# A transformer block pair on one core: the first mixer's projections in a new order

## The chip, the cores and the metric

The program runs on one core of a Trainium2 chip. The metric is the device time of one execution in microseconds; for the kernel before, the median of three runs is 1390.18 us (1381.83 to 1393.23). The engines are PE (matrix products), DVE and ACT (element-wise work), POOL, and SP, which here issues all loads. Each engine works through its own list in order and waits on semaphores where a list says so.

## The reference

512 tokens of width 1024 pass two blocks. The first block is a hybrid mixer, a cross attention to 256 memory rows and a convolutional feed-forward; the second has four small mixers and an MLP. The change lies in the hybrid mixer alone:

```python
def hybrid_mixer(x, w_in, ..., w_out):
    proj = x @ w_in
    ml_qk, ml_v, ml_o, ml_i, ml_f, sw_q, sw_k, sw_v = jnp.split(proj, IN_SPLITS, axis=-1)
    ml_qk = jax.nn.silu(causal_dwconv(ml_qk, ml_conv_w, ml_conv_b))
    ml_q, ml_k = jnp.split(ml_qk, 2, axis=-1)
    h_ml = mlstm(ml_q, ml_k, ml_v, ml_o, ml_i + ml_i_bias, ml_f + ml_f_bias, ml_norm_g)
    h_sw = sliding_window_attention(sw_q, sw_k, sw_v, swa_sinks, rel_bias)
    return jnp.concatenate([h_ml, h_sw], axis=-1) @ w_out
```

The mLSTM has 4 heads of width 128 with an input and a forget gate per head and token. The sliding window has 8 query heads of width 64 on 2 key heads; it works in 4 blocks of 128 tokens, each looking at itself and the block before, with a bias table of 128 x 8 x 256. A softmax with a sink stands in the middle.

## The kernel before

All weights come in 221 chunks of 128 x 1024 fp32 (512 KB). A chunk is loaded into one of 3 stage slots (SP), its high part is cast to fp32r (ACT, `split`, L1023), the rest is subtracted (DVE, `split`, L1377), and a product of fp32 quality is three fp32r products: high x high, high x low, low x high. There are 6 slots for split chunks. A load of chunk i waits for the low part of chunk i-3 (its stage slot), the cast of chunk i for the product of chunk i-6. The tokens are split the same way into `xh` and `xl`, 8 pieces of 128 features (`x_in`).

A class `Plan` writes one list of steps; each engine's program walks this list and does its part of each step. The order in `Plan.mixer_one` is thus the order on every engine. `fill` takes one of 8 PSUM banks in turn and PE waits for whoever read it last; `out` gives it back; `pump` appends `split` steps for up to six chunks ahead. `feat` is one chunk with weights stationary and 512 tokens moving (24 products); `tok_small` and `tok_half` have tokens stationary. `sliding_window` and `mlstm` are generators whose pieces are laid between chunks, one at each `next(side)`.

Names in the order of the list: `in_a` (the sliding window's k, q, and as sixth chunk the 8 gate rows, padded to 128), `in_sv` (its v), `in_qk` (q and k of the mLSTM, 8 chunks), `in_v`, `in_o`, `kv_k` and `kv_v` (the memory's keys and values), `out1` (the output projection). For a window block n: `swa_scores` (PE scores; DVE adds bias and takes the maximum; ACT exponentials), `swa_norm` (DVE), `swa_turn` (PE transposes the probabilities, ACT copies), `swa_pv` (PE product with v). For a chunk of q or k: `conv_qk` (ACT copies and scales, DVE three taps) and `silu_qk`. For a head: `ml_gate` and `ml_score` (PE, then ACT and DVE), `ml_out` (PE), `ml_norm` (DVE, one step on POOL), `ml_turn` (PE). `masks` waits on DVE for the bias table. `tok_full` lays out `out1`: for each of 8 chunks the four token tiles, the last five chunks tile by tile (`tail`).

Of the kernel before, what the change touches and what calls it, by code (L numbers as in the profile page):

```python
# [18 lines left out]
CH = 1024  # L19
# [13 lines left out]
WEIGHTS = [("in_a", 6), ("in_sv", 1), ("in_qk", 8), ("in_v", 4), ("in_o", 4), ("kv_k", 8), ("kv_v", 8), ("out1", 8),  # L33
           ("xq", 8), ("xo", 8), ("up", 44), ("down", 22), ("in2_c", 4), ("in2_a", 4), ("in2_v", 2), ("in2_b", 10),
           ("out2", 8), ("m1", 32), ("m2", 32)]
CHUNKS = [(n, c) for n, k in WEIGHTS for c in range(k)]
CHUNK0 = {n: CHUNKS.index((n, 0)) for n, _ in WEIGHTS}


class Plan:  # L40
# [66 lines left out]
    def tok_full(self, name, nk, early=1):  # L107
        for b in range(8):
# [7 lines left out]
        for k in range(7):  # L116
            split_in(k)
        ahead = 7
        for k in range(nk - TAIL):
            self.need()  # L120
            self.step("full", name, k)
            self.used += 1
            self.pump()
            if k + 7 < nk:
# [46 lines left out]
    def sliding_window(self):  # L171
# [9 lines left out]
        yield  # L181
        for n in range(4):
            self.step("swa_norm", n)
            for _ in range(3):
                yield
# [12 lines left out]
            yield  # L198

    def mlstm(self):  # L200
# [9 lines left out]
        def turned(h):  # L210
            self.fill("ml_t", h)
            self.step("ml_turn", h)
            self.out(("ml_t", h), "ml_y", h + 1)
            if h == 0:
                self.step("first", "out1")

# [4 lines left out]
        for h in range(4):  # L221
            if h:
                turned(h - 1)
# [8 lines left out]
            if h < 2:  # L232
                front(h + 2)
                yield
        yield
        turned(3)

    def mixer_one(self):
        for k in range(8):
            if k in (0, 5, 7):  # L240
                self.pump(1)
# [3 lines left out]
        for j in self.feat("in_a", 6):  # L245
            self.step("in_a", j)
            self.out(("in_a", j), *(("a_out", j + 1) if j < 5 else ("g_in", 2)))
        self.tok_small("in_sv", 0)
        self.step("in_sv")
        self.out(("in_sv", 0), "sv_out", 1)  # L250
        self.pump()
        self.step("gates")
        side = self.sliding_window()
        for j in self.feat("in_qk", 8):
# [4 lines left out]
            if j == 2:  # L259
                self.fill("gate_columns")  # L260
                self.step("gate_columns")
                self.out(("gate_columns",), "gc_out", 1)
            next(side, None)
        self.step("silu_qk", 7)
        self.tok_half("in_v", 0, 4, lambda: next(side, None))
        for t in range(4):
            self.out(("in_v", 0, t), "v_out", t + 1)
        self.step("in_v")
        for k in self.feat_mid("in_o", 4, lambda: next(side, None)):
            self.step("in_o", k)  # L270
            self.out(("in_o", k), "o_t", k + 1)
            next(side, None)
        for _ in side:
            pass
        self.step("ml_setup")
        side = self.mlstm()
# [3 lines left out]
        next(side)  # L280
        for k in self.feat("kv_k", 8):
            self.step("kv_k", k)
            self.out(("kv_k", k), "kt_out", k + 1)
            next(side, None)
        for hf in range(2):
            self.tok_half("kv_v", hf, 2, lambda: next(side, None))
            for t in range(2):
                self.step("kv_v", hf, t)
                self.out(("kv_v", hf, t), "vm_out", 2 * hf + t + 1)
                next(side, None)  # L290
        for _ in side:
            pass
        self.step("x_again")
        self.step("rows", "ln1")
        self.tok_full("out1", 8)
# [260 lines left out]
class Own:  # L556
# [16 lines left out]
    ["st0", "st1", "st2"] + [f"ld_x{k}" for k in range(4)]  # L573
# [3 lines left out]
    + ["mm", "tile_done", "swa_s_full", "swa_t_full", "swa_o_full", "gc_full", "ml_m_full", "ml_s_full", "ml_h_full",  # L577
# [3 lines left out]
    + ["w_hi", "x_hi", "f_hi", "a_own", "a_out", "sv_out", "gate_e", "gate_x", "swa_e", "swa_pt", "swa_y", "qk_u", "qk_y",  # L581
# [5 lines left out]
    + ["w_lo", "x_lo", "f_lo", "v_own", "masks", "ones", "pad", "g_in", "gate_p", "gate_a", "gate_m", "gate_f", "gc_out",  # L587
# [8 lines left out]
def build_program(nc, d, out):  # L596
    plan = Plan()
    with ExitStack() as ctx:
# [35 lines left out]
        th = reg(22, 512)  # L634
# [10 lines left out]
        pad0 = reg(84, 520, 2064)  # L645
# [9 lines left out]
        sel = gb[:, 1, 0:512]  # L655
        gi = gb[0:4, 1, 512:1024]
        ones = gb[0:4, 2, 0:512]
        g3 = gb[0:4, 2, 512:1024]
        sw_mx, sw_nm, sw_sm, sw_es, sw_rr = (st[:, 8 * i:8 * i + 8] for i in range(5))
# [58 lines left out]

        def tile_ready(name, t):
# [11 lines left out]
        def _(e):  # L731
# [9 lines left out]
            def by_weights(b, i, cols, ks):  # L741
# [3 lines left out]
                for k in ks:  # L745
                    if i == 0:
                        q.wait_ge(S["x_lo"], plan.x_at["x", k])
# [5 lines left out]
            def feat(name, j, x, part=None):  # L753
# [4 lines left out]
                if i:  # L758
                    q.wait_ge(S["x_lo"], x)
# [11 lines left out]
            def feat_rest(name, j, x, part=None):  # L771
# [3 lines left out]
                if part != "front":  # L775
                    last.then_inc(S["mm"])

# [53 lines left out]
            def full(name, k):  # L831
                for t in range(4):
                    last = product(name, k, t)
                last.then_inc(S["mm"])
# [34 lines left out]
            def swa_scores(n):  # L869
                lo = 0 if n else 128  # L870
                q.wait_ge(S["a_out"], 5)
                for j in range(2):
                    rows = slice(64 * j, 64 * j + 64)
                    for ip in range(2):
                        b = tiles(fill("swa_score", n, 2 * j + ip)[:], 2)
                        for i in range(2):
                            last = e.matmul(b[:, i, lo:256], swq[rows, 2 * ip + i, tok(n)],
                                            swk[rows, (n - 1) * 128 + lo:(n + 1) * 128], start=True, stop=True)
                        last.then_inc(S["swa_s_full"])

            def swa_turn(n):
                q.wait_ge(S["ld_ident"], 16)
                q.wait_ge(S["swa_p"], n + 1)
                for j in range(2):
                    for kb in ([0, 1] if n else [1]):
                        b = fill("swa_turn", n, j, kb)
                        for i in range(4):
                            last = e.transpose(b[:, tok(i)], L[:, 4 * j + i, tok(kb)], ident[:])
                        last.then_inc(S["swa_t_full"])

            def swa_pv(n):
                b = fill("swa_pv", n)
                q.wait_ge(S["swa_pt"], 4 * n + 2)
                q.wait_ge(S["sv_out"], 1)
# [7 lines left out]
            def ml_gate(h):  # L902
                b = fill("ml_m", h)
                q.wait_ge(S["gate_m"], 1)
                q.wait_ge(S["ld_masks"], 80)
                e.matmul(b[:], sel[0:4, tok(h)], g3, start=True, stop=True).then_inc(S["ml_m_full"])

            def ml_score(h):
                q.wait_ge(S["qk_s"], 5 + h)
# [5 lines left out]
            def ml_out(h):  # L915
                E = Es[h % 2]
                q.wait_ge(S["v_out"], 4)
                q.wait_ge(S["ones"], 1)
# [85 lines left out]
            mine = dict(feat=feat, feat_half=feat_half, feat_rest=feat_rest, tok_small=tok_small, tok_half=tok_half,  # L1004
# [9 lines left out]
        def _(e):  # L1014
# [3 lines left out]
            def split(i):  # L1018
# [4 lines left out]
                e.copy(whi[:, i % NSPLIT, :], stage[:, s, :]).then_inc(S["w_hi"])  # L1023

            def x_in(k):
                q.wait_ge(S[f"ld_x{k // 2}"], 32)
# [7 lines left out]
            def x_from(name, k):  # L1034
                q.wait_ge(S["mm"], CHUNK0[name] + max(0, k - 7))
                if name == "out1":
                    q.wait_ge(S["ml_y" if k < 4 else "swa_y"], k + 1 if k < 4 else 4)
# [7 lines left out]
                e.copy(xh[:, k % 8, :], source[name][:, k, :]).then_inc(S["x_hi"])  # L1045

            def first_in(name):
# [3 lines left out]
                if name == "out1":  # L1051
                    q.wait_ge(S["ml_y"], 1)
# [6 lines left out]
                e.copy(first[:, 0, :], source[name][:, 0, :]).then_inc(S["f_hi"])  # L1059
# [8 lines left out]

            def in_a(j):
                if j < 5:  # L1070
                    q.wait_ge(S["mm"], CHUNK0["in_a"] + j + 1)
# [961 lines left out]
```

## Time and profile before

| what | us |
|---|---|
| median of 3 runs | 1390.18 |
| profiled execution | 1390.49 |
| its span in the trace | 1388.7 |
| PE busy | 1335.8 |
| DVE busy | 737.9 |
| ACT busy | 548.0 |
| out1 begins (PE) | 251.13 |

The span is what the engines' records cover; what lies around it is 1.8 us. A busy share of 96% on PE says that nearly all time is a list of products, but the records of pipelined products overlap, so their cost is read from one start to the next and not from their length. The granted clock of PE is 1.00 (2.4 GHz) or 0.50 (1.2 GHz) in a stretch.

### The profile page before, as it was taken

Reading aid. Unit: us, or ns where it says so; the run is one execution under the profiler, and the core shown is the slowest. Engines: PE = TensorE matmul, PEld = TensorE weight load, DVE = VectorE, ACT = ScalarE, POOL = GpSimd, SP = SyncE. Lnnn points to the kernel's source line nnn. Section 1 sums busy time; section 2 is a strip of 40 time slices with the busy share of each in tenths; the row PEclk is TensorE's granted clock in tenths of the full one; section 3 lists DMA queues with packets and bytes.
Section 4 is the critical chain, followed back from the end, with each engine's and each line's share of the span. In section 5 each row is a group of like instructions: output and inputs, shape, how many; then the busy total and the mean of one; then the engine's idle time right before and its main releaser. Section 6 shows DMA issues by size and latency. Waiting matters only on the chain.

```text
span 1388.7 us, 15947 instructions
## 1 busy us (share of the span) xinstructions
PE 1335.8 (96%) x6476; PEld 1100.2 (79%) x6476; DVE 737.9 (53%) x1049; ACT 548.0 (39%) x908; POOL 7.8 (1%) x8
## 2 busy tenths in 40 slices
PE   6999998999999999999999989998989999999997
PEld 5877786888688888888888788765778888888886
DVE  4486577482537655555533679765373333433323
ACT  3455642323413544444422242476343322323221
POOL 0000001000000000000000000000000000000000
PEclk9999999999999999999999989999999999999999
DMA  7322223623112432323432132111223323333211
GB/s 258 118 77 76 83 70 99 219 77 107 46 46 76 122 91 91 104 94 105 139 105 92 31 124 92 52 55 62 90 76 105 93 93 105 107 105 93 92 60 61
DMA packets 37096, 131.55 MB, mean 95 GB/s; under 512 B 4252, under 2 KB 4892, under 8 KB 36768
## 3 DMA queue, kind: packets, MB, share of 16 engines
q1 hardware_dynamic: 37024, 130.55, 29.2%
q8 instruction: 51, 0.84, 0.2%
q14 instruction: 21, 0.17, 0.1%
HBM read 128.43 MB, written 2.10 MB: 94 GB/s over the span
## 4 chain that ended last, share of the span: by engine, by line
PE 81%; DVE 9%; ACT 5%; issue 2%; DMA 1%; POOL 0%; SPq 0%; DVEq 0%; ACTq 0%; POOLq 0%
PE bank L748 14%; PE bank L749 14%; PE bank L750 14%; PE bank L824 5%; PE bank L825 5%; PE bank L826 5%; PE bank L829 5%; PE bank L827 5%; PE bank L828 5%; DVE wlo L1377 1%; ACT whi L1023 1%; PE bank L958 1%; DVE R L1485 1%; DVE xl L1407 1%; PE bank L788 1%
## 5 line engine op out<-in xcount | busy, mean ns | idle before, releaser
L1377 DVE TENSOR_TENSOR wlo<-stage,whi 128x1024 fp32r<-128x1024 f32 x221 | 269.4, 1224 | 338.6 <-ACT whi L1023 338.6
L748 PE MATMUL bank<-xh,whi 128*128 128x512 f32 (+1 forms) x1152 | 424.3, 368 | 23.4 <-DVE xl L1407 12.0
L749 PE MATMUL bank<-xl,whi 128*128 128x512 f32 (+1 forms) x1152 | 418.1, 363 | 0.0
L750 PE MATMUL bank<-xh,wlo 128*128 128x512 f32 (+1 forms) x1152 | 417.9, 363 | 0.0
L1023 ACT CAST whi<-stage 128x1024 fp32r<-128x1024 f32 x221 | 229.7, 1045 | 242.3 <-PE bank L829 195.7
L748 PEld LDWEIGHTS bank<-xh,whi 128*128 128x128 f32 x1152 | 221.1, 192 | 66.0 <-DVE xl L1407 13.4
L750 PEld LDWEIGHTS bank<-xh,wlo 128*128 128x128 f32 x1152 | 221.0, 192 | 33.2
L749 PEld LDWEIGHTS bank<-xl,whi 128*128 128x128 f32 x1152 | 221.2, 192 | 32.4 <-issue 1.2
L824 PE MATMUL bank<-whi,xh 128*128 128x512 f32 x296 | 116.2, 392 | 0.1
L826 PE MATMUL bank<-wlo,xh 128*128 128x512 f32 x296 | 115.2, 389 | 0.0
L825 PE MATMUL bank<-whi,xh 128*128 128x512 f32 x296 | 115.2, 389 | 0.0
L829 PE MATMUL bank<-whi,xl 128*128 128x512 f32 x296 | 115.2, 389 | 0.0
L827 PE MATMUL bank<-wlo,xh 128*128 128x512 f32 x296 | 115.2, 389 | 0.0
L828 PE MATMUL bank<-whi,xl 128*128 128x512 f32 x296 | 115.2, 389 | 0.0
L1814 DVE TENSOR_TENSOR R<-bank,R 128x512 f32<-128x512 f32 x32 | 22.1, 692 | 96.5 <-ACT R L1350 96.5
L1350 ACT ACTIVATE R<-bank 128x512 f32<-128x512 f32 x32 | 19.1, 598 | 118.6 <-PE bank L750 118.6
L1658 DVE SCALAR_TENSOR_TENSOR R<-R,par 128x512 f32<-128x512 f32 x44 | 33.1, 751 | 60.7 <-ACT R L1206 60.4
L824 PEld LDWEIGHTS bank<-whi,xh 128*128 128x128 f32 x296 | 55.6, 188 | 12.0 <-issue 0.8
L828 PEld LDWEIGHTS bank<-whi,xl 128*128 128x128 f32 x296 | 55.6, 188 | 11.6
L827 PEld LDWEIGHTS bank<-wlo,xh 128*128 128x128 f32 x296 | 55.6, 188 | 11.6
L825 PEld LDWEIGHTS bank<-whi,xh 128*128 128x128 f32 x296 | 55.6, 188 | 11.5 <-issue 0.2
L829 PEld LDWEIGHTS bank<-whi,xl 128*128 128x128 f32 x296 | 55.6, 188 | 11.5
(247 smaller groups left out, 1389.5 us busy)
## 6 DMA issues: line engine op xcount, KB each, us to landing
stage<-in_W_m SPq DMA_DIRECT2D x64, 512.0 KB, 3.5
stage<-in_W_up SPq DMA_DIRECT2D x44, 512.0 KB, 3.5
stage<-in_W_down SPq DMA_DIRECT2D x22, 512.0 KB, 3.5
stage<-in_W_out SPq DMA_DIRECT2D x16, 512.0 KB, 3.6
stage<-in_W_in_a SPq DMA_DIRECT2D x10, 512.0 KB, 3.7
stage<-in_W_in_b SPq DMA_DIRECT2D x10, 512.0 KB, 3.4
stage<-in_W_in_qk SPq DMA_DIRECT2D x8, 512.0 KB, 4.3
stage<-in_W_kv_k SPq DMA_DIRECT2D x8, 512.0 KB, 3.5
```

Of the source, the lines that this page charges most:

```text
L748: e.matmul(b[:, cols], hi[:, k, :], xh[:, k, cols], start=(k == 0), stop=False)
L749: e.matmul(b[:, cols], hi[:, k, :], xl[:, k, cols], start=False, stop=False)
L750: last = e.matmul(b[:, cols], lo[:, k, :], xh[:, k, cols], start=False, stop=(k == 7))
L824: e.matmul(b[0][:], a_hi, hi[:, 0:512], start=(k == 0), stop=False)
L825: e.matmul(b[1][:], a_hi, hi[:, 512:1024], start=(k == 0), stop=False)
L826: e.matmul(b[0][:], a_hi, lo[:, 0:512], start=False, stop=False)
L827: e.matmul(b[1][:], a_hi, lo[:, 512:1024], start=False, stop=False)
L828: e.matmul(b[0][:], a_lo, hi[:, 0:512], start=False, stop=end)
L829: return e.matmul(b[1][:], a_lo, hi[:, 512:1024], start=False, stop=end)
L1023: e.copy(whi[:, i % NSPLIT, :], stage[:, s, :]).then_inc(S["w_hi"])
L1377: e.tensor_tensor(wlo[:, i % NSPLIT, :], stage[:, i % NSTAGE, :], whi[:, i % NSPLIT, :].bitcast(F32), ALU.subtract).then_inc(S["w_lo"])
L1658: e.scalar_tensor_tensor(out=y, in0=u[:, 0:512], scalar=P("fcw", w), in1=y, op0=ALU.mult, op1=ALU.add).then_inc(own.inc())
```

## The change

1. v of the mLSTM, the 8 gate columns and the sliding window's v become one product `tokv` at the very start: 8 chunks of 648 columns (324 KB), tokens stationary, two groups of 264 and 384 columns for each of 4 token tiles, all 8 banks. PE does the high parts first and waits for the low parts later. Of chunks 0 to 2 the loads go between the first token pieces.
2. The gates come out with tokens on partitions; four transposes (`gate_turn`) turn them. The gate product of each head takes an fp32r high and low part in one product of 36 rows, and no longer an fp32 product of 4 rows.
3. q and k come head by head (0, 4, 1, 5, ...), with two buffers each for conv and tanh.
4. The sliding window is taken apart in halves of four heads (`swa_norm n j`, `swa_turn n j`), the scores alternate between the two row halves, and its pieces are laid twice in each `in_qk` chunk. The mLSTM's pieces begin within `in_o`.
5. The memory is loaded after the last silu. `out1` takes the window's rows first; the fourth token tile of its first three chunks comes after the other three tiles, with the last head's transposes between.

The names in the listings: `tokv_out` evicts the first product (ACT v of heads 0, 1 and gates; DVE the rest); `w_lo`, `w_hi` count split chunks, `st0` to `st2` landings, `swa_e` exponentials, `swa_p` normalised halves.

ACT at the end of the first product, in the change. L1112 is the cast of a chunk, L1162 and L1164 the two copies of `tokv_out`, L1169 the copy of `in_a 0`:

```order
L1112 CAST whi<-stage 128x1024 [waits mm,st0]
L1112 CAST whi<-stage 128x1024 [waits mm,st1]
L1162 COPY R<-bank 128x2x128 [waits vt_full]
L1164 COPY R<-bank 128x2x4 [waits gate_z]
L1162 COPY R<-bank 128x2x128 [waits vt_full]
L1164 COPY R<-bank 128x2x4
L1162 COPY R<-bank 128x2x128 [waits vt_full]
L1164 COPY R<-bank 128x2x4
L1162 COPY R<-bank 128x2x128
L1164 COPY R<-bank 128x2x4
L1169 COPY R<-bank 128x512 [waits mm]
```

The casts of chunks 12 and 13 (the first two rows) stand ahead of the first copy; before, none of these copies was there, and v was copied from its banks much later.

DVE from block 1's logits to its first half of normalised probabilities, before (L1456 logits, L1377 low part of a chunk, L1485 conv, L1494 silu, L1471 to L1475 normalisation):

```order
L1456 SCALAR_TENSOR_TENSOR R<-bank,R 128x512 [waits swa_s_full] x3
L1460 TENSOR_REDUCE st<-R 128x8 [waits swa_logit]
L1462 TENSOR_TENSOR st<-st,gb 128x8 [waits v_own]
L1464 TENSOR_SCALAR st<-st 128x8 [waits v_own]
L1466 TENSOR_TENSOR st<-gb,st 128x8 [waits swa_nm]
L1377 TENSOR_TENSOR wlo<-stage,whi 128x1024 [waits w_hi,st0]
L1485 SCALAR_TENSOR_TENSOR R<-R,par 128x512 [waits qk_y,qk_u]
L1485 SCALAR_TENSOR_TENSOR R<-R,par 128x512 [waits v_own] x2
L1494 SCALAR_TENSOR_TENSOR R<-R 128x512 [waits qk_t]
L1471 TENSOR_TENSOR st<-st 128x8 [waits swa_e]
L1473 RECIPROCAL st<-st 128x8 [waits v_own]
L1475 TENSOR_TENSOR R<-R,st 128x2048 [waits v_own]
```

The same in the change (L1566 logits, L1474 low part, L1596 conv, L1606 silu, L1582 to L1586 normalisation, here from the second half's maximum):

```order
L1574 TENSOR_SCALAR st<-st 128x4 [waits v_own]
L1576 TENSOR_TENSOR st<-gb,st 128x4 [waits swa_nm]
L1474 TENSOR_TENSOR wlo<-stage,whi 128x1024 [waits w_hi,st2]
L1596 SCALAR_TENSOR_TENSOR R<-R,par 128x512 [waits qk_y,qk_u]
L1596 SCALAR_TENSOR_TENSOR R<-R,par 128x512 [waits v_own] x2
L1606 SCALAR_TENSOR_TENSOR R<-R 128x512 [waits qk_t]
L1474 TENSOR_TENSOR wlo<-stage,whi 128x1024 [waits w_hi,st0]
L1582 TENSOR_TENSOR st<-st 128x4 [waits swa_e]
L1584 RECIPROCAL st<-st 128x4 [waits v_own]
L1586 TENSOR_TENSOR R<-R,st 128x1024 [waits v_own]
L1596 SCALAR_TENSOR_TENSOR R<-R,par 128x512 [waits qk_y,qk_u]
L1596 SCALAR_TENSOR_TENSOR R<-R,par 128x512 [waits v_own] x2
```

One chunk with its conv and silu still lies between, and now a second chunk's low part too; maxima and normalisation are in halves.

PE around the first transposes of block 1, in the change (L976 transposes, L966 scores, L986 product with v):

```order
L803 MATMUL bank<-xl,whi 128x512
L804 MATMUL bank<-xh,wlo 128x512
L976 MATMUL bank<-ident,R 128x128 [waits swa_p]
L976 MATMUL bank<-ident,R 128x128 x3
L976 MATMUL bank<-ident,R 128x128 [waits swa_logit]
L976 MATMUL bank<-ident,R 128x128 x3
```

Before, the same transposes came four chunks after the scores, now two; the wait is for the first half alone now.

The diff, cut to its core:

```diff
-WEIGHTS = [("in_a", 6), ("in_sv", 1), ("in_qk", 8), ("in_v", 4), ("in_o", 4), ...
+WEIGHTS = [("tokv", 8), ("in_a", 5), ("in_qk", 8), ("in_o", 4), ...
+WIDTH = {"tokv": 648}
+VG = [slice(0, 264), slice(264, 648)]
+QK = [0, 4, 1, 5, 2, 6, 3, 7]
...
     def tok_full(self, name, nk, early=1, late=7, lag=0, between=None):
...
+            if k < lag:
+                self.need(k)
+                if k == lag - 1:
+                    between()
+                self.step("full", name, k, range(3))
+                if k < lag - 1:
+                    continue
...
+                for o in range(lag):
+                    self.step("full", name, o, range(3, 4))
+                    self.used += 1
+                    self.pump()
+                continue
...
     def sliding_window(self):
...
         scores(0)
-        yield
         for n in range(4):
-            self.step("swa_norm", n)
-            for _ in range(3):
-                yield
+            yield
+            yield
+            self.step("swa_norm", n, 0)
+            yield
+            self.step("swa_norm", n, 1)
             for j in range(2):
...
-            self.step("swa_turn", n)
-            yield
+                self.step("swa_turn", n, j)
+                if j == 0:
+                    yield
             if n < 3:
                 scores(n + 1)
+            yield
             self.fill("swa_pv", n)
...
     def mixer_one(self):
+        for t in range(4):
+            for g in range(2):
+                self.fill("tokv", t, g)
+        for k in range(NSPLIT):
+            self.pump(1)
             self.step("x_in", k)
             self.x_split("x", k)
         self.step("masks")
+        for k in range(8):
+            self.step("tokv", k)
+            self.used += 1
+            self.pump(1)
+            if k + NSPLIT < 8:
+                self.step("x_in", k + NSPLIT)
+                self.x_split("x", k + NSPLIT)
+        for t in range(4):
+            self.step("tokv_out", t)
...
+        for j in self.feat("in_a", 5):
             self.step("in_a", j)
+            if j == 0:
+                self.fill("gate_turn")
+                self.step("gate_turn")
...
+        next(side)
+        for j in self.feat_mid("in_qk", 8, lambda: next(side, None)):
             self.step("conv_qk", j)
...
+        self.step("mem_load")
+        sides = [side]
...
+        sides.append(self.mlstm())
+        for k in self.feat_mid("in_o", 4, mid):
...
-        self.tok_full("out1", 8)
+        self.tok_full("out1", 8, 1, 6, 3, lambda: self.ml_turned(3))
...
+            def tokv(k):
+
+                hi, lo = whi[:, k % NSPLIT, :], wlo[:, k % NSPLIT, :]
+                groups = [(t, g) for t in range(4) for g in range(2)]
+                q.wait_ge(S["w_hi"], k + 1)
+                q.wait_ge(S["x_hi"], plan.x_at["x", k])
+                for t, g in groups:
+                    b = fill("tokv", t, g) if k == 0 else bank_of("tokv", t, g)
+                    n = VG[g].stop - VG[g].start
+                    e.matmul(b[:, 0:n], xh[:, k, tok(t)], hi[:, VG[g]], start=(k == 0), stop=False)
+                q.wait_ge(S["w_lo"], k + 1)
...
+                q.wait_ge(S["x_lo"], plan.x_at["x", k])
...
             def swa_scores(n):
...
+                for ip in range(2):
+                    for i in range(2):
+                        for j in range(2):
+                            rows = slice(64 * j, 64 * j + 64)
+                            b = tiles(bank_of("swa_score", n, 2 * j + ip)[:], 2)
...
             def ml_gate(h):
                 b = fill("ml_m", h)
-                e.matmul(b[:], sel[0:4, tok(h)], g3, start=True, stop=True).then_inc(S["ml_m_full"])
+                e.matmul(b[:], selr[:, tok(h)], gsum, start=True, stop=True).then_inc(S["ml_m_full"])
...
+            def tokv_out(t):
+                b = bank_of("tokv", t, 0)
+                q.wait_ge(*tokv_ready(t))
+                e.copy(vaug[:, t, 0:2, 0:128], tiles(b[:, 0:256], 2))
+                q.wait_ge(S["gate_z"], 1)
+                e.copy(gt[:, t, :].rearrange("p (g c) -> p g c", g=2)[:, :, 0:4], tiles(b[:, 256:264], 2)
+                       ).then_inc(S["v_out"])
...
+            def mem_load():
+                q.wait_ge(S["qk_s"], 8)
                 e.dma_start(MT, d["memT"]).then_inc(S["ld_mem"], 16)
```

## Rows read from the trace of the kernel before

**Rows 1.** The page, busy time and share of the span by engine.

```profile
PE 1335.8 (96%) x6476; PEld 1100.2 (79%) x6476; DVE 737.9 (53%) x1049; ACT 548.0 (39%) x908; POOL 7.8 (1%) x8
```

**Rows 2.** Windows: length, busy us (instructions) by engine, PEclk, DMA share, GB/s.

```profile
0.00:10.00 10.00, 2.43 (x6) 1.98 (x7) 3.72 (x5) 4.60 (x6) 0.20 (x4) 1.00 0.83 288
0.00:57.00 57.00, 46.32 (x242) 38.81 (x243) 23.06 (x25) 20.45 (x27) 0.20 (x4) 1.00 0.64 220
57.00:171.00 114.00, 112.27 (x540) 88.00 (x538) 77.47 (x106) 63.32 (x140) 0.00 (x0) 1.00 0.24 74
171.00:251.00 80.00, 72.88 (x426) 61.19 (x425) 54.69 (x133) 31.17 (x57) 7.62 (x4) 0.96 0.31 98
225.50:232.20 6.70, 5.96 (x26) 5.88 (x27) 2.95 (x9) 0.00 (x0) 0.00 (x0) 0.50 0.44 143
```

**Rows 3.** Timeline of PE, 0 to 57: start, us, line, idle before.

```profile
7.57 0.77 PE L748 MATMUL bank<-xh,whi 128*128 128x512 f32 x1 [7.57 <-DVE xl L1383]
...
10.27 0.45 PE L748 MATMUL bank<-xh,whi 128*128 128x512 f32 x1
...
45.94 0.22 PE L788 MATMUL bank<-whi,xh 128*128 128x128 f32 x1
...
56.60 0.45 PE L748 MATMUL bank<-xh,whi 128*128 128x512 f32 x1
```

**Rows 4.** Timeline of SP (DMA issues), 15 to 36.

```profile
18.57 0.43 SPq L1853 DMA_DIRECT2D R<-in_swbias  x1
29.43 0.33 SPq L1840 DMA_DIRECT2D stage<-in_W_in_sv  x1
```

**Rows 5.** Timeline of DVE, 14 to 32.

```profile
25.94 2.29 DVE L1413 TENSOR_TENSOR R<-R,gb 128x2048 f32<-128x2048 f32 x1 [9.71 <-DMA R<-in_swbias]
```

**Rows 6.** Timeline of ACT, 33 to 37.

```profile
34.40 1.05 ACT L1023 CAST whi<-stage 128x1024 fp32r<-128x1024 f32 x1 [13.68 <-DMA stage<-in_W_in_sv]
```

**Rows 7.** Timeline of PE, products of 512 and of 256 columns.

```profile
108.34 0.39 PE L803 MATMUL bank<-whi,xh 128*128 128x512 f32 x1
...
119.00 0.39 PE L805 MATMUL bank<-whi,xl 128*128 128x512 f32 x1
...
182.05 0.28 PE L748 MATMUL bank<-xh,whi 128*128 128x256 f32 x1
...
184.45 0.28 PE L750 MATMUL bank<-xh,wlo 128*128 128x256 f32 x1
```

**Rows 8.** Timeline of PE, scores of block 1, gate product of head 0.

```profile
93.05 2.96 PE L877 MATMUL bank<-R 64*128 64x256 f32 x16
...
171.16 1.12 PE L906 MATMUL bank<-gb 4*128 4x512 f32 x2
172.21 1.13 PE L912 MATMUL bank<-R 128*128 128x512 f32 x2
```

**Rows 9.** Timeline of DVE through block 1 of the sliding window.

```profile
101.77 2.48 DVE L1456 SCALAR_TENSOR_TENSOR R<-bank,R 128x512 f32<-128x512 f32 x4
104.28 2.29 DVE L1460 TENSOR_REDUCE st<-R 128x8 f32<-128x2048 f32 x1
...
112.67 1.23 DVE L1377 TENSOR_TENSOR wlo<-stage,whi 128x1024 fp32r<-128x1024 f32 x1 [5.50 <-ACT whi L1023]
113.84 2.33 DVE L1485 SCALAR_TENSOR_TENSOR R<-R,par 128x512 f32<-128x512 f32 x3
...
117.12 2.29 DVE L1475 TENSOR_TENSOR R<-R,st 128x2048 f32<-128x2048 f32 x1
```

**Rows 10.** Timeline of ACT, exponentials of block 1 and the cast behind them.

```profile
107.01 0.51 ACT L1090 ACTIVATE R<-R,st 128x256 f32<-128x256 f32 x1 [7.86 <-DVE st L1464]
...
110.97 0.19 ACT L1093 ACTIVATE st<-st 128x8 f32<-128x8 f32 x1
...
111.53 1.04 ACT L1023 CAST whi<-stage 128x1024 fp32r<-128x1024 f32 x1
```

**Rows 11.** Timeline of PE, the wait before ml_turn of head 2.

```profile
226.24 1.08 PE L932 MATMUL bank<-ident,R 128*128 128x128 f32 x4 [3.55 <-DVE R L1563]
```

More of the change, by code:

```diff
@@ L31 @@
 NPAR = _o
-WEIGHTS = [("in_a", 6), ("in_sv", 1), ("in_qk", 8), ("in_v", 4), ("in_o", 4), ("kv_k", 8), ("kv_v", 8), ("out1", 8),
+WEIGHTS = [("tokv", 8), ("in_a", 5), ("in_qk", 8), ("in_o", 4), ("kv_k", 8), ("kv_v", 8), ("out1", 8),
            ("xq", 8), ("xo", 8), ("up", 44), ("down", 22), ("in2_c", 4), ("in2_a", 4), ("in2_v", 2), ("in2_b", 10),
@@ L105, in tok_half, with tok_full @@
             self.pump()
-    def tok_full(self, name, nk, early=1):
-        for b in range(8):
+    def tok_full(self, name, nk, early=1, late=7, lag=0, between=None):
+        for b in range(6 if lag else 8):
             self.fill(name, b)
@@ L114, in split_in @@
                 self.x_split(name, k)
-        for k in range(7):
+        for k in range(late):
             split_in(k)
-        ahead = 7
+        ahead = late
         for k in range(nk - TAIL):
+            if k < lag:
[5 more added lines that the diff above has]
+                    continue
+                while ahead < min(nk, 8):
+                    split_in(ahead)
+                    ahead += 1
+                self.fill(name, 6)
+                self.fill(name, 7)
+                for o in range(lag):
[3 more added lines that the diff above has]
+                continue
             self.need()
-            self.step("full", name, k)
+            self.step("full", name, k, range(4))
             self.used += 1
             self.pump()
-            if k + 7 < nk:
+            if ahead <= k + 7 < nk:
                 split_in(k + 7)
@@ L233, in mlstm, with ml_turned @@
                 front(h + 2)
+                if h == 1:
+                    self.step("first", "out1")
                 yield
-        yield
-        turned(3)
-    def mixer_one(self):
-        for k in range(8):
-            if k in (0, 5, 7):
-                self.pump(1)
+            elif h == 2:
+                yield
+            if h < 3:
+                self.ml_turned(h)
+    def ml_turned(self, h):
+        self.fill("ml_t", h)
+        self.step("ml_turn", h)
+        self.out(("ml_t", h), "ml_y", h + 1)
+    def mixer_one(self):
+        for t in range(4):
[3 more added lines that the diff above has]
+            self.pump(1)
             self.step("x_in", k)
@@ L258, in mixer_one, with mid @@
                 self.step("silu_qk", j - 1)
[L259 to L262, printed above, removed]
             next(side, None)
         self.step("silu_qk", 7)
[L265 to L269, printed above, removed]
+        self.step("ml_setup")
+        self.step("mem_load")
+        sides = [side]
+        def mid():
+            for s in sides:
+                if next(s, "end") != "end":
+                    return
+        sides.append(self.mlstm())
+        for k in self.feat_mid("in_o", 4, mid):
             self.step("in_o", k)
             self.out(("in_o", k), "o_t", k + 1)
[L272 to L276, printed above, removed]
+            mid()
         for k in range(2):
@@ L283, in mixer_one @@
             self.out(("kv_k", k), "kt_out", k + 1)
-            next(side, None)
+            mid()
         for hf in range(2):
-            self.tok_half("kv_v", hf, 2, lambda: next(side, None))
+            self.tok_half("kv_v", hf, 2, mid)
             for t in range(2):
@@ L289, in mixer_one @@
                 self.out(("kv_v", hf, t), "vm_out", 2 * hf + t + 1)
-                next(side, None)
-        for _ in side:
-            pass
+        for s in sides:
+            for _ in s:
+                pass
         self.step("x_again")
         self.step("rows", "ln1")
-        self.tok_full("out1", 8)
+        self.tok_full("out1", 8, 1, 6, 3, lambda: self.ml_turned(3))
         self.step("warm", 0)
@@ L829, in product, with full @@
                 return e.matmul(b[1][:], a_lo, hi[:, 512:1024], start=False, stop=end)
-            def full(name, k):
-                for t in range(4):
+            def full(name, k, some):
+                for t in some:
                     last = product(name, k, t)
-                last.then_inc(S["mm"])
+                if 3 in some:
+                    last.then_inc(S["mm"])
             def tail(name, nk, t):
@@ L1058, in first_in @@
                     q.wait_ge(S["cf_y"], 1)
[L1059 removed]
+                e.copy(first[:, 0, :], source_of(name, 0)).then_inc(S["f_hi"])
             def turn(name, t):
```

314 lines of the change are left out of this document (171 added, 143 removed).

## The prediction

> **What bounds the kernel now.** I read the page first, for the busy shares: PE is busy in 1335.8 of 1388.7 us, DVE in 737.9, ACT in 548.0 [rows 1]. Then the windows by stage, to see where PE is not busy [rows 2]: 10.7 us of the first 57, 1.7 of the next 114 (to the end of the sliding window), 7.1 of the 80 with the mLSTM, and there it also ran 6.7 us at a granted clock of 0.50 (1.2 of 2.4 GHz). So the first mixer, to 251 us, is PE work of about 224 us plus waits; behind it nothing moves. The change is worth what PE work it removes, and which waits go and come. For those I read the timelines of PE at the start [rows 3], of SP, DVE and ACT where the bias table lands [rows 4 to 6], and of DVE and ACT through one block of the sliding window [rows 9, 10].
>
> **PE work.** A 512-column product takes 0.227 us from start to start (47 steps in 10.66), a 256-column one 0.120 (20 steps in 2.40) [rows 7], a 128-column one 0.111 (96 from 45.94 to 56.60) [rows 3]. Removed: the gates' chunk and v, 24 + 96 products of 512 columns, 27.2 us, and sv, 10.7. Added: 96 of 264 and 96 of 384 columns; on the line between 0.120 and 0.227 these are 0.123 and 0.173, together 28.5 (ends: all at 0.120, 23.0; all at 0.227, 43.6; the widths lie nearer the lower end). Four small transposes add 0.45. Sum **-9.0**.
> The Trainium skill, "TensorE: Matmul & The Clock Gate", section "Back-to-back issue gap", gives N/2.4 + 2.5 ns from start to start; by it the removed work is 31.3 us, the added 26.4, and this term -4.9 in place of -9.0. The rows for 128 and 512 columns are dearer than it, and I go by the rows.
> The gate product of each mLSTM head was two fp32 records, 1.05 us (171.16 to 172.21) [rows 8]; as one fp32r pass of 512 columns it is 0.23: four times 0.82, **-3.3**. The scores' products now alternate between the two halves of the rows; 16 records took 2.96 us [rows 8]. At best that halves, at worst nothing; I take the half for the three full blocks, since the two halves of the rows share nothing but the queue (each product of a pair writes its own bank): **-4.5**, end 0.
>
> **Start.** PE waited until 7.57 for a 512 KB chunk and two token pieces, then 3.1 us more in three waits for data or low parts [rows 2]. Now the first product needs 324 KB and 256 KB and only the high parts; the data lands at about 4.2, the casts (0.7 + 0.6) end at 5.1. Each piece of the sum over k then has 3.6 us of PE work against 580 KB, some 2 us of transfer at the 288 GB/s of the first 10 us [rows 2], so PE stays fed through k = 7. Gain 2.5 + 3.1. The half clock at the start (products 0.43 apart until 10.27, 1.2 us lost) begins earlier and lasts, I take, 1 us more: **-4.6**. The token product then ends at 5.1 + 28.5 + 2 = about 35.5.
>
> **A new wait behind it.** All eight banks are taken, so in_a 0 needs the ACT copy of the first bank, and in ACT's order this stands behind the cast of chunk 13. That chunk's load waits for the low part of chunk 10, chunk 10's load for the low part of chunk 7, and that stands on DVE behind the bias add, which waits for its 1 MB. It was issued at 18.57 and the add began at 25.94, with the 1 MB of memory ahead of it [rows 4, 5]. Now it is issued about 19.4 with that gone: 24.2. Add 2.3 and memsets: 26.9; low parts of chunk 6 and 7 with their tokens: 29.4; chunk 10 lands 33.3, its low part is done at 35.6; chunk 13 lands 39.3, cast 40.4, copies 41.0. PE waits 5.7 us (ends: 3, if the bias lands at 22; 8, if each landing takes the 5.0 from 29.43 to 34.40 [rows 4, 6]). After the wait of 3.55 at 226.24, PE had a half clock and lost half of 5.96 busy us [rows 2, 11]; here I take 2.5. **+8.2**.
>
> **The sliding window, packed into in_qk.** Before, a block spread over about five steps of one chunk each; now over 2.5 chunks. From the end of scores 1 to the moment PE wants its probabilities lie 4 half chunks and one product with v: 10.9 + 1.0 = 11.9 us. The chain on DVE and ACT: 2.0 of conv and silu still queued; logits 2.48; two half reductions with three small steps each, 3.3; the last four exponentials, 2.1 (eight took 3.96, 107.01 to 110.97); the cast 1.04 behind them [rows 9, 10]; DVE had nothing to do meanwhile, 5.5 us in the row of 112.67 and about 3.4 now. Then low part 1.2, ACT's evictions for conv 0.6, conv 2.3, silu 0.6, another low part 1.15, half a normalisation 1.6. Sum 18.6: PE waits **6.7**. The old rows check the method: 101.77 to 119.41 is 17.6 with the same pieces. For blocks 2 and 3 the PE leg is 12.8 and the chain 18.1 and 18.4: 5.3 and 5.6. For block 0 (128 columns) 8.2 against 11.7: 3.5. That is 21.1; after the three longer waits the half clock costs 6 more, less than three times 3.0 since it covers part of a later wait. **+27**, ends 0 (DVE never late) and +36. The 1.7 us idle of 57 to 171 go: **-1.5**.
>
> **mLSTM.** Its steps now begin in in_o. From ml_out to ml_turn lie 11 to 12 us of PE for heads 0 and 1, 8.9 for head 2, and all of kv_v and three chunks of out1 for head 3; the chain of ml_norm was about 9 (217 to 226.24). So 7.1 idle and 3.0 of half clock go: **-10.1**. Small waits for the in_a copy and the later memory load: +0.9. out1 has the same products in another order; its chunks 6 and 7 are cast after tile 3's first products, 1.4 us apart, with 4 us of other chunks before they are needed: 0. The gates' chain on ACT (about 12 us) lies beside in_a 1 and 2, whose low parts exist: 0.
>
> **Sum.** -9.0 - 3.3 - 4.5 - 4.6 + 8.2 + 27 - 1.5 - 10.1 + 0.9 = +3.1 on the profiled execution's 1390.5, so 1393.6; that execution is 0.3 over the median of 1390.18, so I say **1393**. What the change gains in work and at the mLSTM it gives back in the sliding window.
>
> **Rivals.** (A) PE never waits in the sliding window: the halves of scores and normalisation shorten the chain, and DVE has work of about 19 us a block against 18.9 of PE. For it: equal work; against it: order, since DVE stands still behind the casts on ACT whatever its load. 1393 - 27 = 1366; with half the waits 1379. (B) The other side, slower: the half clock. It decides if 0.50 stays granted for the whole leg from a block's first transposes to the next scores, 6.2 us of PE, and not for a part: three legs at 6.2 more in place of 2 each, +12.6, 1406. For it: the waits come every 25 us and open with small work; against it: after 226.24 the clock was back within 6.7 us. (C) The added products cost 0.227 whatever their width: +15, 1408; the 256-column row speaks against it. (D) The start's wait does not come, the bias being early: 1385.
>
> **Numbers.** Forecast with D 0.59, A and its half 0.26, B 0.12, C 0.03. Runs shown lie within 0.8%, so 1% (14 us) is about the least that counts as a change: below 1376 faster, above 1404 slower. Faster 0.26, same 0.60, slower 0.14. The range takes in most of A's half and B: 1368 to 1406; the forecast's own is 1383 to 1401.
>
> **What would show it.** First matmul near 5.1; a PE wait before in_a 0 near 35 to 41, released by ACT; four waits of 3 to 7 us at the first transposes of a block, released by the probabilities on DVE; DVE idle 3 to 4 us behind the cast of a chunk; out1's first product at 251 + 3 = 254. The forecast is wrong if these four waits are under 2 us each (A), or if PE's clock is at 0.50 for more than 25 us before 254 (B).

## The result, and the profile after

The changed kernel took **1406.9 us** (median; runs 1403.33, 1405.70, 1408.17) against 1390.9 for the kernel before on the same chip (1381.83 to 1393.23): ratio **1.0119, 95% interval 1.0078 to 1.0161**, 16 us slower. One more run of the changed kernel, of 2432 us, was disturbed and is in no ratio. The forecast was 1393 (1368 to 1406), "within 1%" at 0.60. It was wrong: the time lies 0.9 us outside the range, on the slow side, and the first mixer lost 18.4 us where 3 were forecast.

The profiled execution took 1408.17 us, 17.7 more than the profiled one before. Where the difference lies is one row: the first product of `out1`, at 251.13 before, forecast at 254.

```profile
PE 1331.3 (95%) x6452; PEld 1101.4 (78%) x6452; DVE 745.5 (53%) x1091; ACT 549.2 (39%) x919; POOL 7.8 (1%) x8
...
269.53 0.39 PE L910 MATMUL bank<-whi,first 128*128 128x512 f32 x1
```

It is 18.4 us later, so all of the loss is ahead of it in the first mixer; counted from there, the last product comes 0.8 us earlier than before. PE's busy time alone [rows 1] would say the opposite: it fell by 4.5 us. The windows show where PE stood (columns as in [rows 2]; the last one is a stretch of half clock that begins in the last long wait and outlasts it):

```profile
0.00:38.00 38.00, 31.81 (x192) 31.26 (x192) 16.19 (x23) 13.39 (x19) 0.20 (x4) 1.00 0.66 219
...
75.00:190.00 115.00, 96.36 (x437) 71.91 (x436) 73.16 (x129) 56.23 (x141) 0.00 (x0) 0.90 0.20 66
190.00:270.00 80.00, 71.49 (x436) 63.43 (x435) 52.77 (x126) 29.66 (x49) 7.62 (x4) 0.94 0.34 106
205.40:215.60 10.20, 4.95 (x23) 4.97 (x24) 4.49 (x6) 3.44 (x6) 0.00 (x0) 0.50 0.17 53
```

Before, 57 to 171 had 1.7 us of idle PE; now 75 to 190 has 18.6. The waits of PE up to `out1` (engine, line, what it waited for; sum, times, longest) name them:

```profile
PE bank L976 <- DVE R L1586: 18.5, 4, 6.1
PE bank L802 <- ACT R L1164: 8.4, 1, 8.4
PE bank L802 <- issue: 7.7, 1, 7.7
PE bank L840 <- ACT xh L1116: 5.1, 1, 5.1
PE bank L845 <- DVE wlo L1474: 1.0, 1, 1.0
PE bank L1021 <- DVE R L1675: 0.8, 1, 0.8
```

The first row is the four waits in the sliding window, the second the wait before `in_a 0`: both were forecast. The third, **7.7 us before `kv_k 0`**, was not. The fourth is the start (forecast 5.1), the fifth a gap inside the first product, the last the one wait left at `ml_turn`.

### The wait that was not forecast

PE at `kv_k 0`. L1000 is the scores of head 2, L802 the first product with the memory:

```profile
200.11 0.50 PE L994 MATMUL bank<-first 36*128 36x512 f32 x1
200.54 2.42 PE L1000 MATMUL bank<-R 128*128 128x512 f32 x8
210.66 0.55 PE L802 MATMUL bank<-xh,whi 128*128 128x256 f32 x1 [7.69 <-issue]
211.01 0.41 PE L803 MATMUL bank<-xl,whi 128*128 128x256 f32 x1
```

The releaser reads "issue", so the row names nobody; one has to look for who wrote `xh` and `xl` last. ACT in the same stretch (L1239 and L1241 are head 2's exponentials, L1121 the memory's two casts into `xh`):

```profile
203.66 0.40 ACT L1239 ACTIVATE R<-R,st 128x128 f32<-128x128 f32 x1 [2.85 <-DVE R L1622]
203.97 0.56 ACT L1241 ACTIVATE R<-bank,st 128x384 f32<-128x384 f32 x1
...
205.92 1.04 ACT L1112 CAST whi<-stage 128x1024 fp32r<-128x1024 f32 x1
206.85 2.00 ACT L1121 CAST xh<-R 128x1024 fp32r<-128x1024 f32 x2
```

And DVE (L1675 the last part of head 0's `ml_norm`, L1622 the first of head 2's weights, L1487 the memory's low parts):

```profile
201.58 1.11 DVE L1675 TENSOR_SCALAR R<-R,st 128x128 f32<-128x128 f32 x4 [0.91 <-POOL st L2027]
202.61 0.42 DVE L1611 TENSOR_SCALAR R<-R 128x512 f32<-128x512 f32 x1
202.94 0.68 DVE L1622 TENSOR_TENSOR R<-bank,gb 128x512 f32<-128x512 f32 x1
204.56 1.82 DVE L1632 SCALAR_TENSOR_TENSOR R<-bank,R 128x512 f32<-128x512 f32 x4 [0.94 <-ACT R L1241]
207.06 1.23 DVE L1474 TENSOR_TENSOR wlo<-stage,whi 128x1024 fp32r<-128x1024 f32 x1 [0.67 <-ACT whi L1112]
208.20 2.35 DVE L1487 TENSOR_TENSOR xl<-R,xh 128x1024 fp32r<-128x1024 f32 x2
```

The last product that reads the tokens in `xh` starts at 199.79. The casts of the memory into it could follow at once; they start 7 us later, because the plan puts head 2's gate and scores ahead of `mem_in`. ACT stands 2.85 us for a DVE instruction behind a normalisation and POOL's step, then runs the exponentials and a weight cast. The load had nothing to do with it: issued at 168.07, it took 5.6 us. `kv_k 0` then ran at 0.213 per 256-column product where the kernel before has 0.120 [rows 7], 2.3 us more.

### The two forecast places

ACT behind the first product and DVE at the bias add (answers to [rows 5, 6]):

```profile
44.83 1.04 ACT L1112 CAST whi<-stage 128x1024 fp32r<-128x1024 f32 x1 [1.91 <-DMA stage<-in_W_in_qk]
45.78 0.37 ACT L1162 COPY R<-bank 128x256 f32<-128x256 f32 x1
46.04 0.17 ACT L1164 COPY R<-bank 128x8 f32<-128x8 f32 x1
```
```profile
28.24 2.29 DVE L1510 TENSOR_TENSOR R<-R,gb 128x2048 f32<-128x2048 f32 x1 [9.95 <-DMA R<-in_swbias]
```
```profile
37.50 0.34 PE L851 MATMUL bank<-whi,xl 128*128 128x384 f32 x1
46.26 0.79 PE L802 MATMUL bank<-xh,whi 128*128 128x512 f32 x1 [8.43 <-ACT R L1164]
```

The banks are full and done at 37.8, but the two copies that free the first stand behind the cast of chunk 13, whose load hangs, by the stage slots, on a low part behind the bias add.

DVE through block 1 of the window (answers to [rows 9]):

```profile
98.94 1.28 DVE L1566 SCALAR_TENSOR_TENSOR R<-bank,R 128x512 f32<-128x512 f32 x2
...
104.96 0.16 DVE L1576 TENSOR_TENSOR st<-gb,st 128x4 f32<-128x4 f32 x1
108.18 1.23 DVE L1474 TENSOR_TENSOR wlo<-stage,whi 128x1024 fp32r<-128x1024 f32 x1 [3.06 <-ACT whi L1112]
109.83 2.33 DVE L1596 SCALAR_TENSOR_TENSOR R<-R,par 128x512 f32<-128x512 f32 x3 [0.42 <-ACT R L1218]
112.07 0.68 DVE L1606 SCALAR_TENSOR_TENSOR R<-R 128x512 f32<-128x512 f32 x1
112.67 1.22 DVE L1474 TENSOR_TENSOR wlo<-stage,whi 128x1024 fp32r<-128x1024 f32 x1
...
114.21 1.22 DVE L1586 TENSOR_TENSOR R<-R,st 128x1024 f32<-128x1024 f32 x1
```

The chain is the one that was added up: 3.06 us idle behind a cast that stands behind the exponentials, then two low parts, a conv and a silu ahead of the normalisation. PE's four waits show as steps from one start to the next of 3.31, 6.46, 4.57 and 5.76; less the 0.23 of the product in each step they are 3.1, 6.2, 4.3 and 5.5, in sum 19.2. (The view of the waits has 18.5, since it counts from the modelled end of the product before.)

### The profile page after: what moved, and what is told of

Read it like the earlier page. It is cut to its first block, busy times and chain, and to the rows that moved or that the text cites. A ratio compares the mean times of both kernels' runs of the same rounds, so it can differ in the third digit from the quotient of the medians.

```text
span 1406.4 us, 15979 instructions
## 1 busy us (share of the span) xinstructions
PE 1331.3 (95%) x6452; PEld 1101.4 (78%) x6452; DVE 745.5 (53%) x1091; ACT 549.2 (39%) x919; POOL 7.8 (1%) x8
## 4 chain that ended last, share of the span: by engine, by line
PE 82%; DVE 8%; ACT 4%; issue 2%; DMA 2%; SPq 1%; POOL 0%; DVEq 0%; ACTq 0%
PE bank L802 15%; PE bank L804 15%; PE bank L803 15%; PE bank L910 5%; PE bank L911 5%; PE bank L914 5%; PE bank L915 5%; PE bank L912 5%; PE bank L913 5%; PE bank L1047 1%; ACT whi L1112 1%; DVE wlo L1474 1%; DVE R L1596 1%; DVE xl L1504 1%; PE bank L1083 1%
## 5 line engine op out<-in xcount | busy, mean ns | idle before, releaser
L802 PE MATMUL bank<-xh,whi 128*128 128x512 f32 (+1 forms) x1144 | 426.1, 373 | 28.1 <-DVE xl L1504 12.0
L1474 DVE TENSOR_TENSOR wlo<-stage,whi 128x1024 fp32r<-128x1024 f32 (+1 forms) x223 | 268.8, 1210 | 318.0 <-ACT whi L1112 317.7
L1112 ACT CAST whi<-stage 128x1024 fp32r<-128x1024 f32 (+1 forms) x223 | 229.4, 1033 | 233.8 <-PE bank L915 191.7
L802 PEld LDWEIGHTS bank<-xh,whi 128*128 128x128 f32 x1144 | 222.8, 195 | 71.3 <-issue 16.5
L910 PEld LDWEIGHTS bank<-whi,xh 128*128 128x128 f32 x296 | 55.6, 188 | 12.0 <-issue 0.8
L913 PEld LDWEIGHTS bank<-wlo,xh 128*128 128x128 f32 x296 | 55.6, 188 | 11.6
L912 PEld LDWEIGHTS bank<-wlo,xh 128*128 128x128 f32 x296 | 55.6, 188 | 11.5
```

The costliest lines, as they stand in the source:

```text
L802: e.matmul(b[:, cols], hi[:, k, :], xh[:, k, cols], start=(k == 0), stop=False)
L910: e.matmul(b[0][:], a_hi, hi[:, 0:512], start=(k == 0), stop=False)
L912: e.matmul(b[0][:], a_hi, lo[:, 0:512], start=False, stop=False)
L913: e.matmul(b[1][:], a_hi, lo[:, 512:1024], start=False, stop=False)
L1112: e.copy(whi[:, i % NSPLIT, 0:width(i)], stage[:, s, 0:width(i)]).then_inc(S["w_hi"])
L1474: e.tensor_tensor(wlo[:, i % NSPLIT, c], stage[:, i % NSTAGE, c], whi[:, i % NSPLIT, c].bitcast(F32), ALU.subtract).then_inc(S["w_lo"])
```

## The experiments

Each ratio is to the kernel before, run on the same chip. In the expectations, theory Q is the order of the steps: each wait comes from work that the plan puts ahead of what PE needs. "`out1` at" is its first product in the profile (269.53 in the changed kernel).

| kernel | median us | ratio (95% interval) | `out1` at |
|---|---|---|---|
| changed kernel | 1406.9 | 1.0119 (1.0078 to 1.0161) | 269.53 |
| e1: memory's casts first | 1398.0 | 1.0061 (1.0038 to 1.0084) | 260.29 |
| e2: bias add later | 1396.6 | 1.0067 (1.0041 to 1.0092) | 256.79 |
| e3: normalisation earlier | 1381.8 | 0.9948 (0.9920 to 0.9975) | 244.65 |
| e4: all three | 1370.5 | 0.9867 (0.9823 to 0.9911) | 231.66 |
| e5: window not packed | 1387.5 | 0.9975 (0.9964 to 0.9987) | 245.17 |
| e6: scores in twos | 1404.5 | 1.0102 (1.0078 to 1.0126) | 266.54 |

**e1: the memory's casts first.**

```diff
         for k in self.feat_mid("in_o", 4, mid):
             ...
             self.out(("in_o", k), "o_t", k + 1)
+            if k == 3:
+                for i in range(2):
+                    self.step("mem_in", i)
+                    self.x_split("mem", i)
             mid()
-        for k in range(2):
-            self.step("mem_in", k)
-            self.x_split("mem", k)
```

> The memory's split (two casts, two low parts) stands ahead of head 2's gate and scores and not behind them. Theory Q (the 7.7 us wait before kv_k 0 is queue order: ACT's casts stand behind head 2's exponentials, these behind DVE's normalisation of head 0): the wait falls from 7.7 to about 2.8 us, no half clock after it (2.3 us), 7 us less in all than the change. Rival L (the load of the memory is late): the wait stays at 7 to 8 us.

The casts and PE's first product now:

```profile
197.05 0.60 ACT L1229 ACTIVATE R<-bank 128x512 f32<-128x512 f32 x1 [6.16 <-PE bank L805]
197.55 1.98 ACT L1122 CAST xh<-R 128x1024 fp32r<-128x1024 f32 x2
202.77 0.40 ACT L1240 ACTIVATE R<-R,st 128x128 f32<-128x128 f32 x1 [3.25 <-DVE R L1623]
```
```profile
202.24 0.55 PE L803 MATMUL bank<-xh,whi 128*128 128x256 f32 x1 [2.44 <-issue]
```

The wait fell from 7.7 to 2.4 and the stretch of half clock behind it from 10.2 us to 3.4, so that the first 24 products with the memory took 4.35 us in place of 5.17. That is 6.1 of the 9.2 us by which `out1` began earlier. Most of the rest came where the edit changes nothing: the first scores of the window start at 75.56 and not 77.51 (the `in_a 0` wait is 7.7 in this run, with less half clock), and 0.9 more came within the window. The wait's cause is shown: order on ACT and DVE, not the load.

**e2: the bias add behind the first product.**

```diff
-                q.wait_ge(S["ld_bias"], 16)
-                q.wait_ge(S["ld_masks"], 80)
-                e.tensor_tensor(bias, bias, smask...)      # out of masks(), now bias_add()
...
             self.out(("tokv", t, 1), "sv_out", t + 1)
+        self.step("bias_add")
```

> DVE adds the mask to the bias table after the first product's copies; load order is unchanged, the memsets stay early. Theory Q (the 8.4 us wait before in_a 0 is the chain of low parts, loads and casts behind the bias add): the wait falls to about 2 us (the cast of chunk 13 and two copies behind the product's end), the half clock after it goes (2.7), some 9 us less. Rival L (the loads themselves are too slow for the first product): the wait stays over 5 us.

DVE no longer stands 9.95 us for the table; the low parts of the first `in_a` chunks start at 22.95 and 28.35 (in the changed kernel at 33.46 and 36.36), the add runs when nobody waits for it:

```profile
22.95 1.23 DVE L1475 TENSOR_TENSOR wlo<-stage,whi 128x1024 fp32r<-128x1024 f32 x1 [1.16 <-ACT whi L1113]
28.35 3.76 DVE L1475 TENSOR_TENSOR wlo<-stage,whi 128x1024 fp32r<-128x1024 f32 x3 [4.18 <-ACT whi L1113]
...
39.83 2.28 DVE L1517 TENSOR_TENSOR R<-R,gb 128x2048 f32<-128x2048 f32 x1
```

The wait before `in_a 0` is 1.6 us, there is no half clock behind it, the 1.0 us inside the first product is gone too, and `out1` begins 12.7 us earlier (1.1 of it in the cold first 24 products, 5.14 us for 6.27, which the edit does not touch). Shown: 6.8 of the 8.4 us hang on that one instruction of DVE, by way of two stage slots used again (chunk 7's by chunk 10, and that by chunk 13).

**e3: the normalisation ahead of a chunk's conv.** Both halves come one half chunk behind the scores, the product with v one block later, and the cast and low part of the next chunk ahead of the pieces laid behind a chunk (`pump`).

```diff
             yield
-            yield
-            self.step("swa_norm", n, 0)
-            yield
-            self.step("swa_norm", n, 1)
+            if n:
+                pv(n - 1)
+            self.step("swa_norm", n, 0)
+            self.step("swa_norm", n, 1)
+            yield
+            yield
+            if n:
+                yield
             for j in range(2):
...
-            yield
-            self.fill("swa_pv", n)
-            self.step("swa_pv", n)
-            self.out(("swa_pv", n), "swa_y", n + 1)
+        yield
+        pv(3)
...
                 self.step("silu_qk", j - 1)
+            self.pump()
             next(side, None)
```

> Both halves of swa_norm stand one half chunk behind the scores, ahead of the next chunk's conv, and the cast and low part of the next chunk ahead of the scores. Transposes and scores keep their places. Theory Q (order on DVE and ACT makes the four waits): they fall from 19.2 to 0 to 5 us in sum, the clock is at 0.50 for at most one stretch there, 20 us less (12 to 28). Rival W (DVE's work is the bound, about as much as PE's): the waits stay at 12 us or more in sum, since the work is the same.

PE's waits up to `out1`:

```profile
PE bank L810 <- ACT R L1172: 8.2, 1, 8.2
PE bank L810 <- issue: 7.7, 1, 7.7
...
PE bank L984 <- DVE R L1594: 3.2, 1, 3.2
```

Of four waits one of 3.2 us is left (block 2), and one stretch of 3.4 us at the half clock where there were four with 23.9. `out1` begins 24.9 us earlier, 22.0 of it behind the first scores; the other 2.9 came ahead of them (74.65 for 77.51), where the edit changes nothing. DVE did the same instructions in this stage, so it was never short of time, only of order. Which of the edit's three moves did how much was not tested.

**e4: the three together.** The edits are those above.

> The three edits together. If they are independent, 7 + 9 + 20 = 36 us less than the change, about 1372, 1.3% under the kernel before. If DVE's work is the bound (rival W), 1390.

```profile
PE bank L986 <- DVE R L1598: 3.2, 1, 3.2
PE bank L812 <- ACT R L1174: 2.5, 1, 2.5
PE bank L812 <- issue: 2.4, 1, 2.4
```

1370.5 us: 1.3% faster than the kernel before (0.9% to 1.8%), 36 us faster than the change as it was. The gains alone add up to 46.8 us at `out1`, together they are 37.9. Of the 8.9 between, 7.1 lie ahead of the first scores: e1 and e3 begin these 1.95 and 2.86 us earlier than the changed kernel though their edits do not touch that stretch, and e4, at 67.77, 2.3 later than e2. The other 1.8 were not taken apart.

**e5: the window's pieces once a chunk.**

```diff
-        for j in self.feat_mid("in_qk", 8, lambda: next(side, None)):
+        for j in self.feat("in_qk", 8):
```

> The changed kernel with one edit: the sliding window's pieces are laid once in each in_qk chunk (behind it) and no longer twice, so its later pieces slide into in_o and the mLSTM's behind them. A leg between scores and the first transposes then holds about three chunks (16 us and more) in place of 2.5. Theory Q (the four waits at the first transposes come from the packing, the one before kv_k 0 from head 2's exponentials standing ahead of the memory's casts): the waits at the first transposes fall from 19.2 us in sum to under 5 with their half clock of 9, so -20 to -28; the wait before kv_k 0 falls from 7.7 to about 2.5, -7; but the mLSTM's last pieces are pushed together ahead of out1 and each transpose waits there for a normalisation chain of about 9 us: +10 to +20. Sum -10 to -25, so about 1390. Theory W (DVE has too much work for 8 chunks whatever the order) expects the waits to stay where they are and the time at 1405.

```profile
PE bank L802 <- DVE xl L1487: 6.3, 1, 6.3
PE bank L802 <- ACT R L1164: 6.2, 1, 6.2
...
PE bank L976 <- DVE R L1586: 3.2, 2, 1.7
...
PE bank L910 <- DVE xl L1492: 3.0, 1, 3.0
```
```profile
252.43 0.53 PE L910 MATMUL bank<-whi,xh 128*128 128x512 f32 x1 [3.01 <-DVE xl L1492]
```

Half a hit. The waits at the transposes fell from 18.5 to 3.2 us as expected: without the packing they are nearly gone, as they are in e3 with it. But the wait before the memory's first product stayed at 6.3, not 2.5: now the last block's eight exponentials stand in front of the casts instead of head 2's. And the mLSTM, pushed behind, gives back not 10 to 20 us but about 2 at its transposes and products and 4.9 inside `out1`, most of it the wait of 3.0 above, 7 us after its first product, and the stretch of 3.4 us at half clock behind it. The table's 245.17 therefore makes e5 look too good; it is 24.4 us earlier there and 17.9 at the end of the profiled execution. The two misses roughly cancel in the time. Two different pieces of side work between the last product on the tokens and `mem_in` have now cost 7.7 and 6.3 us, so it is the place that is dear, not head 2.

**e6: the scores in twos.**

```diff
                 for ip in range(2):
-                    for i in range(2):
-                        for j in range(2):
+                    for j in range(2):
+                        for i in range(2):
```

> The changed kernel with one edit: the products of the scores take the two row halves one after the other (two products of one half, then two of the other) instead of in turn. Theory R (products on different row halves overlap when they stand in turn): a full block of 16 records goes from 1.93 us to between 2.5 and 3.1, block 0 from 1.09 to about 1.5, together +2 to +4 us of PE work; the waits behind them shorten by none of it, since the probabilities start from the scores' end; time 1409 to 1411. Rival: the gain came from the banks being written in turn, and any order that changes banks is as quick: 1.93 stays, 1407.

A full block (16 records) in the changed kernel, then in e6; before it was 2.96 [rows 8]:

```profile
95.06 2.00 PE L966 MATMUL bank<-R 64*128 64x256 f32 x16
```
```profile
91.22 2.10 PE L966 MATMUL bank<-R 64*128 64x256 f32 x16
```

Theory R as it was written (2.5 to 3.1) failed, and so did its price. (`out1` is 3.0 us earlier than in the changed kernel, but 2.6 of that had come before the first scores, 74.95 for 77.51, where the edit changes nothing.) But the rival does not hold either: the kernel before changes the bank every two products just as e6 does, and takes 2.96. What e6 has and the kernel before has not is a change of row half every two products in place of four; besides, in e6 PE waits for all four banks ahead of the first product, and in the kernel before for each bank between the products. These two were not tested apart. In the changed kernel the second record of a pair starts 0.007 us after the first and the pair takes 0.216; in the kernel before nine of the fifteen steps between records are 0.21 or more. So the halves do overlap, and a run of two products on one half hardly hinders it; with runs of four, and the waits for banks between, most of them do not overlap. A run of three was not tried.

## Why the forecast was wrong, step by step

The terms as they were forecast, and as the trace of the changed kernel has them:

| term | forecast | measured |
|---|---|---|
| PE work | -9.0 | -8.8 |
| gate product | -3.3 | -2.5 |
| scores | -4.5 | -4.0 |
| start | -4.6 | -3.0 |
| wait before `in_a 0` | +8.2 | +11.1 |
| sliding window | +27 | +28.1 |
| small idle in it | -1.5 | -1.5 |
| mLSTM | -10.1 | -9.3 |
| **"Small waits ... and the later memory load"** | **+0.9** | **+10.0** |
| sum | +3.1 | +20.1 |

The scores are measured from a block's first record to the next product's start, which takes in part of what PE waits there in the kernel before; by the records alone they are -3.4. The measured sum is 1.7 above the 18.4 by which `out1` moved; that rest is in no row that I can name. Of the 17.0 us between the two sums, 9.1 are the last term.

**The step that failed** is the last term. It priced the memory by its load, which was early enough, and never followed the queues that the memory's casts share. The chain of the window was written out instruction by instruction, the one in front of `kv_k 0` not at all, though the change moves the mLSTM's pieces exactly there. It is 7.7 us of wait and 2.3 of half clock. With the casts first (e1) the time is 1398, inside the range and inside 1%; the 6.1 us that are surely of this edit would do for that too (1401).

**Mis-sized.** The bias table: the 4.8 us from issue to use assumed that removing the memory's 1 MB would speed it up. It was issued at 20.27 (0.9 later than taken) and used at 28.24, 8.0 us after, no faster than the 7.4 of before [rows 4, 5]. From there the 4.0 us (28.24 for 24.2) went through the stage slots and grew: chunk 10 was cast at 38.06 (landing taken at 33.3), chunk 13 at 44.83 (39.3), and PE began at 46.26 for 41.0. The start: the cold first 24 products took 6.27 us where 3.60 is their later pace, 2.7 lost and not 2.2 (4.96 to 6.23 us in the experiments' profiles, so about 1 us of this differs from one execution to the next); and one step of 1.30 was left in chunk 6, ahead of its low parts, about 1.1 over a product's pace; the other two parts came as forecast (first product at 5.05). The gate product: one record of 0.43 from its start to the next, not 0.23. The half clock in the window: 8.9 us, not 6. Two sums were also added up wrongly, by 0.2 us each: the chain of block 1 comes to 18.4 by its own terms and not 18.6, and from 35.5 to 41.0 are 5.5 us and not 5.7.

**Right.** The chain method: 21.1 us of waits forecast, 19.2 came (3.1, 6.2, 4.3, 5.5 against 3.5, 6.7, 5.3, 5.6 in the order of the blocks), released by the instruction named and with DVE idle 3.06 us behind the cast named. Products of 264 and 384 columns came at 0.121 and 0.179 (0.123 and 0.173 taken), so the added work is 96 x 0.300 = 28.8, with 0.35 for the four small transposes. The rule of the Trainium skill ("TensorE: Matmul & The Clock Gate", section "Back-to-back issue gap") gives 0.1125 and 0.1625 for them and -4.9 for the term; the page states it for the isolated gap and says that it counts too little for few columns. The measured steps are above it by 8 to 10%, and the measured term is -8.8. The waits of the mLSTM went: 0.8 us is left of 7.1.

**The rivals.** A (the window never waits) is refuted by the first row of the waits. C is refuted by the two steps just given, D by the 8.4 us. B is refuted as a mechanism, though its 1406 is the time that came: the window's half clock cost 2.9 more than forecast, not 12.6. The sign that I had set for it, more than 25 us at 0.50 before `out1`, came true (44.4 us in six stretches) and says little of B, since each stretch begins while PE still waits; a time at half clock has to be counted in products run in it.

## What to carry to other kernels

Where in-order queues feed one busy engine, price a moved step at every engine that it has instructions on, and write out the chain for each point where the busy engine will want something: the unpriced one is the one that costs. Work that only has to be done some time (a bias add, a probability's normalisation) belongs behind what the busy engine needs next, work that reopens a shared buffer (the memory's casts) at the very front; the same instructions in another order were worth 36 us here. If a change makes many moves, look at each wait that it leaves before judging it: three local edits turned 1.2% slower into 1.3% faster.

## What the runs showed of the hardware

- PE's granted clock fell to 0.50 (1.2 GHz) around waits in this stage, and stayed so in stretches of 3.4, 6.8 or 10.2 us. With the wait of 3.55 in the kernel before and with all of 4.1 to 6.3 us the stretch was 6.8 us; with waits of 7.7 to 8.4 it was 6.8 or 10.2, both at waits of 7.7 (e1, e2). Waits of 3.0 to 3.2 (e3, e4, e5) came with 3.4 us. Waits of 2.4 to 2.9 came with 3.4 us or with none, at the same place too: in block 0 of the window 2.92 (changed kernel) and 2.90 (e1) with it, 2.91 (e2) and 2.82 (e6) without. With waits of 1.5 to 2.3 there was none. A long wait thus cost 2.2 to 2.7 us more than itself, one with a stretch of 3.4 us about 1.5 (24 products in 4.35 us in e1, where 24 times 0.120 is 2.9).
- fp32 products of 64 rows overlap in pairs when they use different halves of the rows: 16 records in 2.0 us in turn and 2.1 in twos, against 2.96 where four products of one half come first (there PE also waits for a bank every two products).
- A 1 MB transfer that shared the start with weights and tokens took 8.0 us to its use, with 1 MB less ahead of it than before, when it took 7.4. The memory's 1 MB, issued at 168.07, took 5.6.
